# A two-layer diffusion trunk step in split fp32: the matmuls of the conditioning weights in another order and in other buffers

## What is computed

```python
mod = jnp.einsum('bd,de->be', jax.nn.silu(cond), p['w_ada']) + p['b_ada']
sh1, sc1, g1, sh2, sc2, g2 = jnp.split(mod[:, None, :], 6, axis=-1)
h = _rms(x, p['g_norm1']) * (1 + sc1) + sh1
u = h @ p['w_in']                       # four mixers and 4 x 1024 gate columns
...
x = x + g1 * (merged @ p['w_out'])
h2 = _rms(x, p['g_norm2']) * (1 + sc2) + sh2
x = x + g2 * _conv_ffn(h2, p['w_up'], p['conv_w'], p['conv_b'], p['w_down'])
```

## Time and profile before

| | |
|---|---|
| median of 3 runs | 1375.12 us (1372.86, 1375.12, 1375.39) |
| the profiled execution's own time | 1374.23 us |
| its span | 1372.4 us |
| mean granted TensorE clock | 0.983 |
| TensorE busy (matmuls) | 1314.1 us, 96% of the span, 7832 instructions |
| VectorE, ScalarE, GpSimd busy | 54%, 44%, 7% |
| chain that ended last, by engine | PE 84%, DVE 7%, DMA 3%, ACT 2%, issue 2%, SPq 1% |
| moved by DMA | 198.13 MB, mean 144 GB/s |

### The profile page before, as it was taken

How to read it: one execution, slowest core, us unless ns; L and a number is a source line. 1 busy time by engine, 2 the same in 40 slices (tenths; PEclk the granted TensorE clock), 3 DMA queues, 4 the chain that set the end, 5 groups by cost and what they waited for, 6 DMA issues and landing times.

```text
span 1372.4 us, 19334 instructions
## 1 busy us (share of the span) xinstructions
PE 1314.1 (96%) x7832; PEld 1209.5 (88%) x7832; DVE 741.4 (54%) x1260; ACT 597.9 (44%) x1000; POOL 89.4 (7%) x77
## 2 busy tenths in 40 slices
PE   4899999999999999999989999999999899999999
PEld 1887978888989999999979788788889799999999
DVE  0525256444847777763353442654366577777532
ACT  2445544543345444442333554545432544444321
POOL 1000000001810000000100000000044100000000
PEclk9899999999999999999999999999999999999999
DMA  9531244454333333347644222445443243333443
GB/s 372 211 119 61 72 162 161 155 184 154 107 134 112 123 123 124 123 150 271 223 190 138 87 77 80 169 166 181 157 142 116 96 138 123 125 125 124 134 138 123
DMA packets 53545, 198.13 MB, mean 144 GB/s; under 512 B 6416, under 2 KB 6832, under 8 KB 52944
## 3 DMA queue, kind: packets, MB, share of 16 engines
q1 hardware_dynamic: 53136, 196.19, 40.8%
q0 software_dynamic: 320, 0.69, 0.2%
HBM read 194.59 MB, written 2.27 MB: 143 GB/s over the span
## 4 chain that ended last, share of the span: by engine, by line
PE 84%; DVE 7%; DMA 3%; ACT 2%; issue 2%; SPq 1%; POOL 0%; POOLq 0%; DVEq 0%; ACTq 0%
PE bank L1032 24%; PE bank L1034 23%; PE bank L1033 23%; PE bank L1016 2%; DMA w_raw<-stream 2%; DVE wide L949 2%; DVE w_lo L729 1%; PE bank L1247 1%; PE bank L1267 1%; PE bank L1237 1%; SPq L301 1%; ACT w_hi L430 1%; ACT wide L430 1%; DVE act_lo L777 1%; DVE wide L771 1%
## 5 line engine op out<-in xcount | busy, mean ns | idle before, releaser
L729 DVE TENSOR_TENSOR w_lo<-w_raw,w_hi 128x1024 fp32r<-128x1024 f32 x258 | 315.4, 1223 | 370.0 <-ACT w_hi L430 369.7
L1032 PE MATMUL bank<-act_hi,w_hi 128*128 128x386 f32 x1424 | 497.2, 349 | 17.7 <-DVE act_lo L777 11.9
L1034 PE MATMUL bank<-act_hi,w_lo 128*128 128x386 f32 x1424 | 486.9, 342 | 0.0
L1033 PE MATMUL bank<-act_lo,w_hi 128*128 128x386 f32 x1392 | 475.9, 342 | 0.0
L430 ACT ACTIVATE w_hi<-w_raw 128x1024 fp32r<-128x1024 f32 x258 | 270.6, 1050 | 164.1 <-DMA w_raw<-stream 164.1
L1032 PEld LDWEIGHTS bank<-act_hi,w_hi 128*128 128x128 f32 x1424 | 272.5, 191 | 31.8 <-issue 29.1
L1034 PEld LDWEIGHTS bank<-act_hi,w_lo 128*128 128x128 f32 x1424 | 272.4, 191 | 0.0
L1033 PEld LDWEIGHTS bank<-act_lo,w_hi 128*128 128x128 f32 x1392 | 266.9, 192 | 1.0
L1032 PE MATMUL bank<-mlp_hi,w_hi 128*128 128x386 f32 x352 | 119.2, 339 | 0.0
L1033 PE MATMUL bank<-mlp_lo,w_hi 128*128 128x386 f32 x352 | 119.1, 338 | 0.0
L1034 PE MATMUL bank<-mlp_hi,w_lo 128*128 128x386 f32 x352 | 118.9, 338 | 0.0
(11 more groups left out here) (202 smaller groups left out, 1450.0 us busy)
## 6 DMA issues: line engine op xcount, KB each, us to landing
w_raw<-stream SPq DMA_DIRECT2D x258, 512.0 KB, 3.3
ada<-ada_w SPq DMA_DIRECT2D x68, 512.0 KB, 3.4
ada_head_a<-ada_w SPq DMA_DIRECT2D x16, 512.0 KB, 5.2
ada_head_b<-ada_w SPq DMA_DIRECT2D x12, 512.0 KB, 9.4
time_consts<-time_consts SPq DMA_DIRECT2D x2, 1920.0 KB, 15.5
params<-params SPq DMA_DIRECT2D x2, 926.0 KB, 11.4
x<-x_in SPq DMA_DIRECT2D x1, 1544.0 KB, 9.9
y_out<-x SPq DMA_DIRECT2D x1, 1158.0 KB, 6.6
```

What stands on the lines that cost most here:

```text
L729: V.tensor_tensor(wlo[s][:, :], raw[s][:, :], whi[s][:, :].bitcast(F32), ALU.subtract).then_inc(lo_ready, 1)
L1032: T.matmul(out, wb[s][0][:, w, :], hi[k], start=first and k == 0, stop=False)
L1033: T.matmul(out, wb[s][0][:, w, :], lo[k], start=False, stop=False)
L1034: ins = T.matmul(out, wb[s][1][:, w, :], hi[k], start=False, stop=last and k == n - 1)
```

## The change

The 96 modulation units get one order over both layers (`ADA_ORDER`), scale before shift for the first norm, and these places:

- layer 0: 16 at the start as before; 24 in attention (one in each of steps 0 to 7, 9 to 16 and 18 to 23, two more as the tail); 8 behind the squares of the second norm, from eight buffers of their own (`norm_ada`).
- in layer 0's MLP, for layer 1: 8 in the up projections (one after every four dense units, the scale), 8 in the down projections (one after every three dense units, two after the seventh three): the first halves of shift and of first gate.
- layer 1: 8 behind the squares of the first norm from `heada` (the other halves), 16 in attention (steps 0, 2, ... 14 and 16 to 23), 8 behind the squares of the second norm.

The ring of two buffers stays for the others. The modulation of the first gate and of the second shift move to attention steps 8 and 17 in layer 0; in layer 1 shift is read inside the first norm, first gate right behind it, second shift in step 15. At the layer boundary the dense weights run on as one stream: slots are counted over both layers, so units 0 to 3 of layer 1 load as the last units of layer 0 are used.

```diff
+CHUNK = (1, 0, 2, 3, 4, 5)
+ADA_ORDER = ([(0, q, k) for q in range(6) for k in range(KD)]
+             + [(1, 0, k) for k in range(KD)]
+             + [(1, q, k) for q in (1, 2) for k in range(4)]
+             + [(1, q, k) for q in (1, 2) for k in range(4, KD)]
+             + [(1, q, k) for q in range(3, 6) for k in range(KD)])
+ATTN_ADA = (HEAD, 72)
+NORM_ADA = (40, 88)
+UP_ADA, DOWN_ADA, HOLE_ADA = 48, 56, 64
+RING = [*range(16, 40), *range(48, 64), *range(72, 88)]
+ADA_STEP = ([1] * 8 + [0] + [1] * 8 + [0] + [1] * 6, [1, 0] * 8 + [1] * 8)
+ADA_TAIL = (2, 0)
+MOD_STEP = ({8: 2, 17: 3}, {15: 3})
+def mod_bank(layer, q):
+    return (6, 0) if (layer, q) == (1, 2) else (7, 2 * P * (q % 2))
...
 SyncE
+            def load_ada(n):
+                c = RING[n]
+                sp.wait_ge(ada_done, max(RING[n - 2] + 1, HEAD) if n >= 2 else HEAD)
+                sp.dma_start(ada[n % 2][:, :], ada_w[c:c + 1, :, :]...).then_inc(ada_loaded[n % 2], 16)
...
+                    n = l * UNITS + i * SLOTS + u - SKIP
+                    if n >= SLOTS:
+                        sp.wait_ge(unit_done, FROM + SKIP + n - SLOTS + 1)
...
+                last = RING.index(ATTN_ADA[l]) + sum(ADA_STEP[l]) + ADA_TAIL[l]
                 for i in range(STEPS):
+                    for _ in range(ADA_STEP[l][i]):
+                        if ring < last:
+                            load_ada(ring)
+                            ring += 1
                     load_unit(first_step + SLOTS + i)
+                for u in range(first_step + SLOTS + STEPS, O0 + SLOTS):
                     load_unit(u)
+                sp.wait_ge(gated_ready, FROM + (l + 1) * KD * 4)
+                for n in range(KD):
+                    load_norm_ada(l, n)
+                for u in range(O0 + SLOTS, P0 + SLOTS):
+                    load_unit(u)
...
+                    for n, u in enumerate(range(D0 + SLOTS, UNITS + SLOTS)):
                         load_unit(u)
...
 VectorE, norm
+                    if n == 0 and l == 0:
+                        modulation(0, 0)
+                        modulation(0, 1)
+                        scales(sc1, 8, "g1")
                     if n == 0:
                         split(0)
                         split(1)
...
+                        if k == 0 and n == 0 and l > 0:
+                            modulation(l, 1)
...
                 norm(0)
+                if l > 0:
+                    modulation(l, 2)
...
-                    if i == 12:
-                        modulation(1, 16, 32)
+                    if i in MOD_STEP[l]:
+                        dve.wait_ge(mla_roped, FROM + (l + 1) * 4)
+                        modulation(l, MOD_STEP[l][i])
...
 (between up and down projections)
+                if l < DEPTH - 1:
+                    dve.wait_ge(head_par_loaded, 16 * l + 32)
+                    modulation(l + 1, 0)
+                    scales(sc1, 8, "g1")
...
 TensorE
+            def ring_ada(c0, c1):
+                for c in range(c0, c1):
+                    at, q, k = ADA_ORDER[c]
+                    n = RING.index(c)
+                    if k == 0 and (at, q) != (1, 2):
+                        pe.wait_ge(mod_read, FROM + 6 * at + q)
+                    pe.wait_ge(ada_loaded[n % 2], 16 * (n // 2 + 1))
+                    modulate(ada[n % 2], c)
...
+                else:
+                    square_sums(0)
+                    hole_units()
                 pair(0, 0, HI, LO, lambda k: pe.wait_ge(norm_lo, l * 2 * KD + k + 1))
...
+                    c = ATTN_ADA[l] + sum(ADA_STEP[l][:i])
+                    ring_ada(c, c + ADA_STEP[l][i])
+                c = ATTN_ADA[l] + sum(ADA_STEP[l])
+                ring_ada(c, c + ADA_TAIL[l])
                 turn(STEPS - 1)
...
                 square_sums(1)
-                ada_units(HEAD + sum(ADA_STEP) + ADA_TAIL, ADA_E)
+                norm_units(l)
...
+                    if l < DEPTH - 1 and 1 <= i < 1 + KD:
+                        ring_ada(UP_ADA + i - 1, UP_ADA + i)
...
+                        at = i * 4 + d
+                        if l < DEPTH - 1 and at < KD - 1:
+                            ring_ada(DOWN_ADA + at, DOWN_ADA + (KD if at == KD - 2 else at + 1))
```

More of the change, by code:

```diff
@@ L53 @@
 UNITS = D0 + U_DN
-SLOT_USES = [len(range(s, UNITS, SLOTS)) for s in range(SLOTS)]
+SKIP = 0
 ADA = 48
-HEAD, ADA_M, ADA_S, ADA_E = 16, 32, 40, 48
+HEAD = 16
 HEAD_PARTS = ((0, 4), (4, 8), (8, 12), (12, 14), (14, 16))
-ADA_STEP = [1, 1, 2] * 4 + [0] + [1] * 11
-ADA_TAIL = 1
+CHUNK = (1, 0, 2, 3, 4, 5)
[4 more added lines that the diff above has]
+             + [(1, q, k) for q in range(3, 6) for k in range(KD)])
+ADA_AT = {unit: c for c, unit in enumerate(ADA_ORDER)}
+ATTN_ADA = (HEAD, 72)
[5 more added lines that the diff above has]
+MOD_STEP = ({8: 2, 17: 3}, {15: 3})
 STRIP = 32
@@ L99, with __init__ @@
 HC = 2 * PAST + HEADS * HD + PAST + PAST
[L102 removed]
+def mod_bank(layer, q):
+    return (6, 0) if (layer, q) == (1, 2) else (7, 2 * P * (q % 2))
 class Links:
[L108 to L110 removed]
+    def __init__(self, eng, sem):
+        self.eng, self.sem, self.n = eng, sem, 0
     def __call__(self, ins):
@@ L116, in wait @@
     def wait(self, but=0):
-        self.eng.wait_ge(self.sem, self.layer * self.per + self.n - but)
+        self.eng.wait_ge(self.sem, self.n - but)
 def program(nc, stream, ada_w, params, caches, consts, time_consts, x_in, cond,
@@ L254, in program @@
         ada_loaded = [sem(f"ada_loaded{s}") for s in range(2)]
+        norm_ada_loaded = [sem(f"norm_ada_loaded{n}") for n in range(2)]
+        hole_ada_loaded = [sem(f"hole_ada_loaded{n}") for n in range(2)]
+        shift_ready, gate2_ready = sem("shift_ready"), sem("gate2_ready")
         head_loaded = [sem(f"head_loaded{n}") for n in range(len(HEAD_PARTS))]
@@ L359, in _ @@
                         load_unit(P0 + SLOTS + j, i)
+                    if l < DEPTH - 1 and 2 <= i < 2 + KD:
+                        load_ada(ring)
+                        ring += 1
+                    if l < DEPTH - 1 and i == 1:
+                        sp.wait_ge(gate2_ready, l + 1)
+                        sp.dma_start(par[:, 0:HEAD_PARAMS], params[l + 1:l + 2, :, 0:HEAD_PARAMS].rearrange("a p n -> (a p) n")
+                                     ).then_inc(head_par_loaded, 16)
                 if l < DEPTH - 1:
-                    for n, u in enumerate(range(D0 + SLOTS, UNITS)):
+                    for n, u in enumerate(range(D0 + SLOTS, UNITS + SLOTS)):
                         load_unit(u)
@@ L366, in _ @@
                             sp.wait_ge(mlp_lo, FROM + 1 + (l + 1) * FB)
-                        if n == HEAD - 1:
-                            sp.wait_ge(ada_done, (l + 1) * ADA)
-                        if 1 <= n <= HEAD:
-                            load_head(n - 1, slice(l * HEAD + n - 1 + HEAD, l * HEAD + n + HEAD))
+                        if 2 <= n < 2 + KD:
+                            load_hole_ada(n - 2)
+                        if n % 3 == 2 and n < 18:
+                            load_ada(ring)
+                            ring += 1
                 else:
@@ L384, in _ @@
             nc.gpsimd.memset(small[:, 0:1], EPS).then_inc(eps_ready, 1)
-            own = Links(pool, pool_own, KD * 2 + 6)
+            own = Links(pool, pool_own)
             for l in range(DEPTH):
-                own.layer = l
-                own.n = 0
                 def sum_squares(n):
@@ L695, in _ @@
                             square(k, 1)
-                assert own.n == ACT_OWN, own.n
         @block.vector
@@ L929, in _ @@
                 attention_out(STEPS - 1)
-                modulation(2, 32, 40)
+                modulation(l, 4)
                 scales(sc2, 32, "g2")
@@ L969, in _ @@
                 norm(1)
-                modulation(3, 40, 48, 256)
+                modulation(l, 5)
                 for i in range(FB // 2):
@@ L1002, in _ @@
                     residual(d, d % 4, 40, x2_ready)
-                assert own.n == DVE_OWN, own.n
         @block.tensor
@@ L1447 @@
             s[D0 + q::3, :, 0:part.shape[2] * P] = part.reshape(KD, P, -1)
-        m = w["w_ada"][l].reshape(KD, P, 6, 8, 4, STRIP).transpose(2, 0, 1, 4, 3, 5).reshape(ADA, P, UNIT)
-        own = DEPTH * HEAD + l * (ADA - HEAD)
-        ada[l * HEAD:(l + 1) * HEAD] = m[:HEAD]
-        ada[own:own + ADA - HEAD] = m[HEAD:]
+        m = w["w_ada"][l].reshape(KD, P, 6, 8, 4, STRIP).transpose(2, 0, 1, 4, 3, 5).reshape(6, KD, P, UNIT)
+        for c, (at, q, k) in enumerate(ADA_ORDER):
+            if at == l:
+                ada[c] = m[CHUNK[q], k]
         def put(name, a):
```

167 lines of the change are left out of this document (91 added, 76 removed).

## The result

Eleven runs each: 1377.85 us after (1375.63 to 1379.53) against 1374.48 before, ratio 1.0026, interval 1.0018 to 1.0035. The change made the kernel slower by about a quarter of a per cent; the forecast had been 1374.2, no change, with slower at 0.28. The profiled execution has a span of 1377.7 against 1372.4, so its trace has 5.3 us to explain where the medians have 3.4: about 2 of it belong to these two executions and not to the change.

A forecast was written before the change was run, and what follows sets the result against it. TensorE was taken to bound the kernel, pausing only at a few seams, so units in its stream are paid. The terms summed to -0.2 us, from a mean of 1374.4 to 1374.2 us, range 1369.5 to 1379.3.

The forecast's parts named there:

- the load that is late at step 23: End of layer 0's attention: third unit in a row waits for its load, 3.1 plus 0.43 us, +3.5.
- the second norms: Eight own buffers leave no load wait in each layer's second norm: -2.2 us in layer 0, -2.8 in layer 1.
- the boundary: Layer boundary: first norm starts sooner, but two modulations return to VectorE's chain, -2.3 us, bounds -1.5 and -3.6.
- the gate's modulation in step 8: Layer 0's attention: the first gate's modulation adds to VectorE's chain, which binds steps 8 and 9, +0.66 us.
- The start: Start of layer 0: modulation now comes before the weight splits, -1.0 us, bounds 0 and -1.2.
- the eight loads: Eight loads, 4.2 MB, before the output projections use an idle queue and cost 0.
- the second rival: Eight loads hold up O0+4, a dense unit of the output projections: +5, 1379 us; chance 0.13.
- Twelve units leave: Layer 1's attention: units removed, those of steps 1, 2, 3, 5, 7 gained at full price; -5.5 us in all.
- so a unit costs 0.83 - 0.18 = 0.66 us: Layer 0's MLP: price of a single modulation unit among dense units, giving +10.3 us for the MLP.
- a second pause of 3.1 us just ahead should cost one such stretch more: End of layer 0's attention: step 23's wait brings one more stretch at 1.2 GHz, +1.0 us, between 0 and 1.7.
- The third rival: Pauses at step 23 and the boundary, or MLP seams, bring more time at 1.2 GHz: 1377.5 us; chance 0.15.
- units in a pause are free: Whole kernel: only units in TensorE's stream cost time; 56 in the stream and 40 in pauses, before and after.

The follow-up runs named there:

- e10: The changed kernel timed once more with no edit: 1377.57 us, ratio 1.0039 to the kernel before.
- e9b: The kernel before with six modulation units of layer 1's early attention steps left out and not computed: 1371.89 us, ratio 1.0001.
- e3: Changed kernel, layer 1's attention: three units moved from steps 10, 17, 19 to 3, 5, 7, second shift's modulation to step 11: 1377.89 us, ratio 1.0032.
- e5: Changed kernel with each of the 16 MLP units replaced by one 128x128 matmul over a quarter of its columns: 1371.82 us, ratio 0.9997.
- e6: Changed kernel with six of the down projections' eight units moved to the layer boundary pause, 14 units there: 1373.46 us, ratio 1.0001.
- e4: Changed kernel with the 16 units in layer 0's MLP standing in 8 pairs: 1374.0 us, ratio 1.0008.
- e7: Changed kernel with the last units of both attentions behind step 23's values, VectorE modulating behind the branch's low parts: 1367.46 us, ratio 0.9964.
- e8: Changed kernel with e3's steps, e6, e7, five pairs in the MLP and the first gate's modulation in step 10: 1357.62 us, ratio 0.9895.
- e11: e8 with one more unit of layer 1's attention moved from step 0 to step 1: 1359.39 us, ratio 0.9913.

## Why the prediction was wrong

*Right by their own steps:* the load that is late at step 23 (3.5 forecast, 3.6 seen); the second norms (-2.2 and -2.8 against -2.0 and -2.7); the boundary (-2.3 against -2.5), with both modulations in VectorE's chain; the gate's modulation in step 8 (0.66 forecast, some 0.5 seen). The start, -1.0 forecast, gave -0.8 in one profile and -0.2 in the other.

*Right with little to spare:* nothing was lost at O0+4 to the eight loads, as both traces need the same 77.5 us from the last turn to the squares of the second norm. But the room was not what the forecast worked out. The eight are issued from 372.32 on and the last lands at 387.16, that is 4.2 MB in 14.8 us or 283 GB/s, which is in the range where the second rival feared a loss. O0+4 lands behind them at 388.42, and that is 385.2 on the scale of the kernel before, half a us ahead of the rival's limit of 385.7.

*The failed step: "Twelve units leave. At full price go step 1 (-0.57), 2 (-0.43), 3 (-0.57), 5 (-1.0), 7 (-0.57)".* Layer 1's attention gave 1.0 us (1.1 in e10) in place of 5.5. Steps 8, 9, 12 and 13 had been looked up for who sets their pace, and were right. Steps 1 to 7 had not: the price of a full TensorE was taken for them. What was not asked is how late the next one, VectorE's rotation, is behind TensorE. The runs show: with the units gone the rotary matmuls wait, 0.75 us in step 3, 0.30 more in step 5, 0.83 in step 7, and take back most of what steps 1 to 5 gave. The unit of step 7 has no such wait behind it, and its -0.57 came in full (-0.67). In e9b only 1.1 of 2.8 were left, and in e3 two of the three units put back were given back at the waits. The rest is the clock: layer 1's attention after has 10 us at the lower level in both of its profiles, of which the stretch behind step 5's wait is the longest; that of the kernel before has 3.4. In the profiles of e5 and e6, which have this stage unchanged and also only 3.4 us of it, the stage gives 3.9. So of the 4.5 missing some 1.6 are waits and some 2.9 the clock, in these executions. Of those 2.9, 1.6 come back behind the attention, where a stretch of before is absent.

*A term mis-sized: "so a unit costs 0.83 - 0.18 = 0.66 us".* It is 0.77 and makes 11.9 us in place of 10.3. The split into work and seams was right (e4, e5), but the first dense matmul behind a seam is longer by 0.11, and the row that was used ended at its start.

These two, 1.6 and 1.6, have no clock in them and are nearly as large as the 3.6 us between the forecast and the median. That the sizes are so close is in part luck, since the 1.0 that the forecast had put in for the clock is not seen at its place, and stretches elsewhere fill it up. This third term, *"a second pause of 3.1 us just ahead should cost one such stretch more"*, failed: between 325 and 345 us each profile with the pause for VectorE has one stretch, with the pause at step 23 or without it. The third rival gave the right time, 1377.5, but not the reason: over the runs of e10 the clock of the changed kernel was no lower than that of the kernel before.

Its largest omission lies one step earlier, where it says what bounds the kernel: *"units in a pause are free"* was counted by units and not by room. The boundary and the two attention ends had 4.4 and 2.4 us left over; with them filled (e6, e7, e8) the idea of the change pays.

Open: why the 1.0 us that e3's trace shows doesn't show in its time, and what decides where a low-clock stretch falls. No run took the clock apart by itself.

## What to carry to other kernels

Price a place for small work by two numbers from the trace: what the seams cost around it, measured to the second instruction behind it, and how far the next engine in the chain is behind; where that one is nearly late, taking work away gives a wait and no time. Count pauses by the idle time left in them, not by what stands in them, and fill them before the dense stream is cut. Where work of another matmul form must go into a dense stream, group it: two units cost 1.2 us in place of 1.54. And work out the room of a transfer from the rate that a run shows for it: the eight loads ran at 283 GB/s, not at the 381 of the start.

## What the runs showed of the hardware

- Going from the 128x128 form to 128x32 and back costs 0.34 us in a dense stream; a change from the dense matmuls' type to f32 in the same form costs nothing that shows (e5).
- Four matmuls of 32 columns of weights run side by side: 7 ns between their starts, and the four take as long as one of the full form (0.43 us for 256 columns in f32, e5).
- Pauses and the clock. In all ten profiles with the wait of some 2.4 us at the end of layer 0's attention, the granted clock from 325 to 345 us averages 0.91; in the three with two units in that wait (e7, e8, e11) it is 1.00. From 700 to 740 us it is 0.91 nine times and 0.96 once with the longer pause, and 1.00, 1.00 and 0.96 in the three with 14 units. With it e7 and e8 came out 3 to 6 us faster than their sums; e6, with the boundary filled alone, did not. That is a coincidence seen in 13 profiles, not a cause taken apart.
